# One more gate from seven products, and four pieces of VectorE's work at other places of its order

## The reference, cut to what matters

```python
h = rmsnorm(x, attn_norm_w); z = h @ w_in
hq, hf, hi, hg, cq, ckv, kr, gate_a, gate_b = split(z)
o_a = hgrn2_mixer(hq, hf, hi, hg, ...)      # chunkwise scan, decays from cumulated gates
o_b = mla_mixer(cq, ckv, kr, positions, ...)
y = sigmoid(gate_a) * (o_a @ w_branch_hgrn) + sigmoid(gate_b) * (o_b @ w_branch_mla)
x = x + y @ w_out
x = x + hierarchical_moe(rmsnorm(x, ffn_norm_w), ...)   # top-1 group, top-2 experts in it
```

```python
score = sum over index heads of relu(iq @ ik.T / 8) * iw    # [256 queries, 256 keys], causal
top_val, top_idx = top_k(score, 64)                          # the 64 best keys of each query
p = softmax(scores of dq with the chosen dk); yb = p @ (chosen dv)
```

## Time and profile before

| | |
|---|---|
| median of three runs | 1583.83 us |
| the profiled execution | 1583.95 us, its span 1582.2 us |
| TensorE busy | 1262.6 us (80%) |
| VectorE busy | 552.8 us (35%) |
| ScalarE busy | 201.4 us (13%) |
| chain that ended last | PE 54%, DMA 40%, DVE 5% |
| mean granted TensorE clock | 0.899 |

### The profile page before, as it was taken

One profiled execution on the slowest core, in us unless ns is written; L12 is line 12 of the kernel. 1 busy time (PEld: TensorE's weight loads), 2 busy tenths in 40 slices (PEclk: granted clock), 3 DMA queues, 4 the chain that ended last, 5 costly groups with the idle time before them and its releaser, 6 DMA issues.

```text
span 1582.2 us, 20568 instructions
## 1 busy us (share of the span) xinstructions
PE 1262.6 (80%) x9054; PEld 797.0 (50%) x9054; DVE 552.8 (35%) x943; ACT 201.4 (13%) x413; POOL 0.5 (0%) x5
## 2 busy tenths in 40 slices
PE   9999999999756846756656665675676999999998
PEld 8967988854313412212212221221221488999985
DVE  5788666732000100101001010010010497798522
ACT  1102033020000000000000000000000211135411
POOL 0000000000000000000000000000000000000000
PEclk9999999999978968878878878877878999999999
DMA  9443165589999999999999999999999654434240
GB/s 365 156 164 130 65 220 226 208 356 426 438 431 436 427 436 437 433 429 441 431 432 436 431 439 432 432 439 431 432 437 425 286 213 159 161 113 167 108 160 27
DMA packets 20565, 507.00 MB, mean 320 GB/s; under 512 B 4240, under 2 KB 4368, under 8 KB 6544
## 3 DMA queue, kind: packets, MB, share of 16 engines
q1 hardware_dynamic: 20208, 505.70, 76.5%
q10 hardware_dynamic: 288, 0.26, 0.0%
HBM read 504.91 MB, written 1.05 MB: 320 GB/s over the span
## 4 chain that ended last, share of the span: by engine, by line
PE 54%; DMA 40%; DVE 5%; issue 1%; ACT 0%; SPq 0%; DVEq 0%; ACTq 0%
DMA ring<-in_experts 37%; PE psP L1317 12%; PE psP L1370 11%; PE psP L753 10%; PE psP L1368 6%; PE psP L801 4%; DMA arena<-in_experts 2%; PE psA L816 2%; DVE arena L1981 2%; PE psP L1477 1%; PE psB L1694 1%; DVE ring L1981 1%; PE psB L1303 1%; PE psA L732 1%; PE psP L1417 0%
## 5 line engine op out<-in xcount | busy, mean ns | idle before, releaser
L1981 DVE TENSOR_TENSOR X<-X,psA 128x512 f32<-128x512 f32 x66 | 45.3, 687 | 695.2 <-PE psA L816 681.0
L753 PE MATMUL psP<-arena 128*32 128x512 f32 x1024 | 150.4, 740 | 133.9 <-DMA arena<-in_experts 133.8
L753 PE MATMUL psP<-ring,arena 128*32 128x512 f32 x1024 | 150.7, 742 | 131.7 <-DMA ring<-in_experts 131.7
L753 PEld LDWEIGHTS psP<-ring,arena 128*32 128x32 f32 x1024 | 38.2, 132 | 239.6 <-issue 235.8
L753 PEld LDWEIGHTS psP<-arena 128*32 128x32 f32 x1024 | 35.9, 132 | 242.2 <-DMA arena<-in_experts 123.5
L1370 PE MATMUL psP<-arena,ring 128*128 128x128 f32 x944 | 111.4, 276 | 1.9 <-DVE ring L1981 1.9
L1370 PEld LDWEIGHTS psP<-arena,ring 128*128 128x128 f32 x944 | 108.1, 192 | 3.4 <-DVE ring L1981 2.5
L1317 PE MATMUL psP<-ring,arena 128*128 128x512 f32 (+2 forms) x240 | 85.9, 515 | 0.0
L801 PE MATMUL psP<-arena 128*32 128x512 f32 x512 | 66.5, 678 | 19.1 <-DMA arena<-in_experts 17.7
L801 PE MATMUL psP<-ring,arena 128*32 128x512 f32 x512 | 65.5, 663 | 19.3 <-DMA ring<-in_experts 17.9
L1981 DVE TENSOR_TENSOR arena<-arena 128x1024 f32<-128x1024 f32 (+6 forms) x103 | 79.2, 798 | 1.5
(11 more groups left out here) (349 smaller groups left out, 1381.4 us busy)
## 6 DMA issues: line engine op xcount, KB each, us to landing
arena<-in_experts SPq DMA_DIRECT2D x7, 4096.0 KB, 21.3
ring<-in_experts SPq DMA_DIRECT2D x7, 4096.0 KB, 22.9
ring<-in_u_gl SPq DMA_DIRECT2D x6, 2048.0 KB, 8.2
ring<-in_u_hq SPq DMA_DIRECT2D x2, 2048.0 KB, 23.4
ring<-in_u_hv SPq DMA_DIRECT2D x2, 2048.0 KB, 11.2
ring<-in_u_hg SPq DMA_DIRECT2D x2, 2048.0 KB, 8.8
ring<-in_u_ga SPq DMA_DIRECT2D x2, 2048.0 KB, 8.7
ring<-in_u_gb SPq DMA_DIRECT2D x2, 2048.0 KB, 8.7
```

Source lines behind the costliest of these rows:

```text
L753: mm = pe.matmul(z[j * CAP:(j + 1) * CAP, :], x[:, 4 * half + k, j * CAP:(j + 1) * CAP], held[c % 4][:, k // 2, j, (k % 2) * 512:(k % 2 + ...
L1981: return dve.tensor_tensor(o, a, b, op)
```

## The change

```diff
-FIRST = ["hq0", "hq1", "hv0", "hv1", "hg0", "ga0", "gb0", "gb1", "wa0", "wa1", "wb0", "wb1"]
+FIRST = ["hq0", "hq1", "hv0", "hv1", "hg0", "ga0", "ga1", "gb0", "gb1", "wa0", "wa1", "wb0", "wb1"]
...
-    before = {"cl": "hg0", "hg1": "ga0", "ga1": "gb0", "gb0": "gb1"}
+    before = {"cl": "hg0", "hg1": "ga0", "ga0": "ga1", "ga1": "gb0", "gb0": "gb1"}
...
     p.append(("halves", "ob", ""))
+    late("wb0")
     p.append(("gated", "wa1", ""))
     p.append(("mnorm", 0, ""))
     sums("wb1")
-    late("wb0")
     proj("wb0")
...
     sums("mq")
+    p.append(("topk", 0, ""))
     proj("mv")
...
     sums("mk")
+    p.append(("topk", 1, ""))
     proj("dg")
...
     soft(6)
-    p.append(("topk", 0, ""))
     p.append(("normal", 6, ""))
     proj("xq")
-    turn(6, 7, "xg", then=[("topk", 1)], after="gl0")
-    turn(7, 8, "gl0", then=[("topk", 2)], after="gl1")
-    turn(8, 3, "gl1", then=[("topk", 3)], after="gl2")
+    turn(6, 7, "xg", then=[("topk", 2)], after="gl0")
+    turn(7, 8, "gl0", then=[("topk", 3)], after="gl1")
+    turn(8, 3, "gl1", after="gl2")
...
         first_sums = {"hq0": w_spare, "hq1": w_10, "hv0": w_spare, "hv1": w_10, "hg0": w_spare, "ga0": w_10,
-                      "gb0": w_spare, "gb1": w_apart,
+                      "ga1": w_spare, "gb0": w_apart, "gb1": w_spare,
...
-            last_used = {"hv0": "hq0", "hv1": "hq1", "hg0": "hv0", "ga0": "hv1", "gb0": "hg0", "wb0": "wa0", "wb1": "wa1"}
+            last_used = {"hv0": "hq0", "hv1": "hq1", "hg0": "hv0", "ga0": "hv1", "ga1": "hg0", "gb1": "ga1", "wb0": "wa0", "wb1": "wa1"}
...
-                    if arg == "gb1":
+                    if arg == "gb0":
 
                         wait_full(dve, ("cnorm", 0))
...
                     if n == 0:
+                        dve.memset(suf[:, :, :], 1.0)
                         link(dve.memset(hattn[:, :, :, :], 0.0))
...
-                        link(dve.memset(suf[:, :, :], 1.0))
                         tt(lq[:, :, :], hq[:, :, :], pre[:, :, :], ALU.mult)
```

## The result

The changed kernel took 1593.47 us in the median of four runs (1592.79 to 1595.6), the kernel before 1583.12 in runs beside it: ratio 1.0069, interval 1.0057 to 1.0081. It is 10.35 us slower; 8.5 was forecast. The profiled execution took 1595.6 us, the longest of the four; its span is 11.6 us longer than that of before.

The account below looks back on a forecast made before the run. TensorE was taken to be bound by VectorE's releasing instructions outside the expert stream, with front delays carried 1:1. Front +3.95 and choices +4.55 made +8.5 on 1583.95, so 1592.4 us; range 1587.5 to 1595.5.

Parts of the forecast that it names:

- Sums of ga1, 3.53 us; the wait of 3.98: Between cnorm and late of ga0: three sums add 3.53 us, so the wait at ga0's last product grows from 0.45 to 3.98.
- The clock behind it, +1.7: Behind the longer wait at ga0's last product the granted clock falls to 0.50, costing +1.7 us (bounds 0 and 1.7).
- Rival A: At ga0 the clock stays at 2.4 GHz behind the wait; total 1590.7 us; chance 0.15.
- The wait of 0.85 in ga1: Level 6: ga1's last product waits 0.85 us for late of ga1, clock left out as moving both engines alike.
- The memset, -0.1: Level 0: moving the suf memset saves only a link, -0.1 us (bounds 0 and -0.45).
- wb0, -0.65 and not -1.26: wb0's 1.26 us wait goes, but wb1 then waits for wb0's third merge operation; net -0.65 us.
- mq and mk, +2.1 and +2.05: Choices 0 and 1 ahead of the merges of mv and dg exceed slacks of 1.27 and 1.55 us: waits 1.93 and 1.9.
- rival E: Clock falls also at mq and mk, or at ga1's 0.85 wait: up to 1.7 us each, 1594 to 1596; chance 0.08.
- Dense stretch, +0.4: Soft-max chunks: longer choices 2 and 3 add 1.1 us, the 0.68 wait goes, net +0.4 (bounds -2.4 and +1.1).
- B: Late of ga0 and merges of mv and dg: VectorE's waits swallow the added work; 1582.1 us, not slower; chance 0.04.
- C: The first region's release is not what holds mq and mk; total 1588.2 us; chance 0.06.
- D: The dense stretch gives back its waits, as a whole choice leaves VectorE's queue; total 1589.6 us; chance 0.05.

Follow-up runs that it names:

- experiment 1: Kernel before with only the ga1 part of the change (seven products, its sums with ga0, buffers exchanged): 1589.09 us against 1582.59, ratio 1.0041.
- experiment 5: Changed kernel with choices 0 and 1 inside the merges of mq and mk, behind the third operation: 1587.27 us against 1583.11 of before, ratio 1.0028.
- experiment 4: Changed kernel with the three sums of ga1 a level earlier, behind those of ga0: 1587.6 us, ratio 1.0034 to before.
- experiment 7: Kernel before with only the suf memset moved ahead of that of hattn, unlinked: 1583.83 us in one time.
- experiment 3: Kernel before with only the late operation of wb0 moved as in the change: 1582.97 us against 1582.59, ratio 0.9998.
- experiment 6: Kernel before with choice 0 alone moved, in two halves ahead of the merges of mv and dg: 1583.46 us, ratio 1.0002.
- experiment 2: Kernel before with only the four choices moved as in the change: 1590.51 us, ratio 1.005.

## Why the prediction was right, and where it was off

- **What bounds the kernel.** Right. The waits lie where a releasing operation came late, and each moved one to one: 3.53 us more work gave 3.53 more wait, and gb0 carried it on. The stream came with it: between the two profiles the products of the two waits of the earlier trace rows stand 2.6 us apart (402.60 and 405.24, 412.17 and 414.83), which is 4.9 - 0.6 less the 1.7 of the start-up.
- **Sums of ga1, 3.53 us; the wait of 3.98.** Right to the hundredth.
- **The clock behind it, +1.7.** Right in kind, too small. The product itself lost 1.73, and the low clock still held over the 64 small matmuls of level 6: from 157.72 to 159.58 there are 1.86 us, where before it was 1.13, so 0.73 more and 2.46 in all. Rival A is out: the clock fell in all five profiles that have this wait (three of the changed kernel, experiments 1 and 5). The row from the expert stage priced the one group behind the wait and not what follows it; the clock stayed low for 5 to 6 us in each of the five.
- **The wait of 0.85 in ga1.** 0.18, 0.28 and 0.34 us in the three profiles. The prediction had the clock move both engines alike. It did not: counted from the start of ga0's last product, ga1's first six products ended 2.5 us later than in experiment 4, where the clock stayed, and late of ga1 ended 2.0 us later. That this and the term above nearly cancel is luck. Without a fall the wait is 0.74 (experiment 4), so the rest of the working for it was right.
- **The memset, -0.1.** Measured -0.13 (experiment 7). The Trainium skill, "VectorE: DVE Perf Modes", section "Zero memsets can be issued as uint32 (trn2)", gives one cycle an element, which is an estimated 3.2 us for the 3072 elements of the other memset at its 0.96 GHz. The trace agrees: 0.59 + 2.62 = 3.21.
- **wb0, -0.65 and not -1.26.** Right: -0.60, and the new wait is at the named product, released by the named operation (experiment 3).
- **mq and mk, +2.1 and +2.05.** The mechanism and its waits were right (1.93 and 1.9 forecast, 1.92 and 1.89 measured), and experiments 5 and 6 show the slack itself. The step that failed is the clock: the prediction took from one row of 2.47 us that a shorter wait doesn't lower it, and put rival E at 0.08. E is what happened at mq and mk, +1.7 each, 3.4 of the sum. The one row was one throw, and the same trace had others that fell behind 2.76 us and one that stayed behind 2.96; length alone did not sort them.
- **Dense stretch, +0.4.** Right in each part: 1.74 became 2.49, 0.51 came new, 0.68 went. Rivals B, C and D are out: the waits are there, mq and mk do wait for the release, and the dense stretch gave nothing back.
- **The sum.** 8.5 forecast. By the table the change itself is 4.9 - 0.6 + 3.85 + 3.8 + 0.4 = 12.35 in executions where the clock falls at both places, and of the 3.85 over the forecast 3.4 are rival E. The three profiled executions, all with both falls, took 1594.24 to 1595.6 us, which is where E stood (1594 to 1596). The medians are only 10.35 apart (9.0 to 12.8 by the interval), since the other three executions took 1592.79 to 1594.03; whether the clock fell less often in them no trace shows. So that the median lies within 2 us of the forecast is in part luck. Experiments 1 and 2 alone make 6.5 + 7.9 = 14.4, more than the whole; their intervals (from 4.4 and 5.9) leave room for it, and the scatter of the clock is a likely reason, not a shown one.

## What to carry to other kernels

A change of VectorE's order is priced by the operation that releases the other engine: what stands ahead of it costs its length less the slack, what stands behind it is free as far as VectorE waits there. So before moving work, find the next release behind the new place and ask on which side of it the work can go; the same choices cost 6 us on one side and nothing on the other. A wait made longer is dearer than its length when the clock falls behind it, and the price runs on as long as the clock stays low. In these traces that happened from 1.74 us on, and not every time: give it a chance, not a threshold, and take more than one profile.

## What the hardware showed that was not expected

- The granted clock behind equal waits differs from execution to execution. It fell in 11 of 14 waits of 1.89 to 1.92 us and in 3 of 8 of 2.48 or 2.49 us (the seven of the table and experiment 5, where it fell), in all five of 3.98, and in 2 of 4 of 1.74 or 1.75 us (in the dense stretch of experiments 3 and 7; not in before and not in experiment 1). At the last wait of the expert stage, 1.83 to 3.26 us in the 14 profiles, it fell behind 1.99 and 3.26 and not behind the other 12, of up to 2.98. So a longer wait did not always make the fall more likely; but these are different places, and what TensorE did ahead of them differs too.
- At mq, mk and ga0 a fall cost 1.7 us on the product behind it. In ga0 the clock stayed low past that product, over small matmuls, and the fall cost 2.46 us in all.
- The first products of the kernel took 7.17 to 7.98 us in 13 profiles and 9.06 in that of before, with the same instructions: up to 1.9 us between two profiles that no change made.
